# One recurrent branch on one core: unpadded products, a state in two buffers, and rows loaded ahead

## The chip, the core and the metric

The kernel is one program on one core of a Trainium2 chip. TensorE (PE in the profile) multiplies, VectorE (DVE), ScalarE (ACT) and GpSimd (POOL) do the rest, and SyncE (SP) issues most DMA transfers. The metric is the device time of one execution in microseconds (us); lower is better. The kernel before takes 3548.88 us, the median of 3 runs (3548.25 to 3555.68).

## The reference, cut to what matters

Two transformer-like blocks run one after the other. The change touches one branch of the first block, a recurrence over 1024 tokens with 8 heads of 64 columns. Each head keeps a 64x64 state:

```
def step(state, inp):                     # wkv7_scan, for each token
    r_t, w_t, k_t, kk_t, a_t, v_t = inp
    sa = einsum('bhvk,bhk->bhv', state, -kk_t)
    state = (state * w_t[:, :, None, :]
             + sa[..., None] * (kk_t * a_t)[:, :, None, :]
             + v_t[..., None] * k_t[:, :, None, :])
    return state, einsum('bhvk,bhk->bhv', state, r_t)
# around it: token shift, decay = exp(-exp(w_log)), a and g from small low-rank products,
# kk = normalised k*k_k, and behind it a group norm per head, a bonus term and the gate g
```

## The kernel before, in words

The program runs its phases one after the other, with a barrier between them: input projection, `rwkv` (this branch), attention, mixing, experts, and the second block. Only `rwkv` is changed, lines 1384 to 2017.

`rwkv` takes the 1024 tokens in 8 tiles of 128, and each tile as two chunks of 64. In a chunk the recurrence is solved in closed form: scores between the scaled rows of the chunk (`score`, L1897), then the inverse of a triangular 64x64 matrix for each head and chunk by squarings and blocks (`prod`, L1905: the names M, N, X, Z, XT, IN), then four steps with the state that must be done chunk after chunk: `state_rows` (L1858, L1859), `state_solve` (L1867), `state_step` (L1879, L1880) and `state_out` (L1887 to L1889). Behind them stand the group norm and the output on DVE (`centred`, `variance`, `output`).

The order is written out by hand for each engine. `body(t)` computes the scores and the inverse of tile t, and lays between them the state steps of tile t-1 (each of them for chunk 0 and for chunk 1) and the front work of tile t+1 (`lora_turn`, `lora_w`, `lora_a`, `lora_gate`, `sums`, `ends` on PE, with `decays` and `scale` on DVE and `exps` on ACT). Each engine runs its list in order and waits on step counters. `each_tile` makes body 0, then a hardware loop of 3 turns with two bodies each (tiles 1 to 6), then body 7; behind that the four state steps of tile 7 stand alone.

Four things matter for the change. The matmuls of `state_rows` and `state_out` contract over all 128 partitions: the state lies block-diagonally in `Sbd` with zeros between two heads, and the masked scores `Km`, `QB` and `QK` are 128 wide with zeros in the other chunk's half. DVE makes those masked scores with two 64-partition instructions each (L1730). SP loads the rows of tile t+2 behind the store of tile t-1's output, which waits for the end of that tile's norm (L1454 to L1466), and ACT reads the rows with `lora_in` (L1491) near the head of the next body. And ACT reloads its function table where two functions do not share one (ACT_TABLE_LOAD, 1.28 us each).

Of the kernel before, what the change touches and what calls it, by code (L numbers as in the profile page):

```python
# [15 lines left out]
P = 128  # L16
# [1344 lines left out]
CH = 64  # L1361
# [26 lines left out]
def rwkv(nc, xs_d, out, masks_d, g):  # L1388

    at, flat = rwkv_masks()  # L1390
    with Phase(nc, "rwkv") as ph:
# [13 lines left out]
        be, ka, vv, gg, lg, bg = (two(n, [P, RW]) for n in "be ka vv gg lg bg".split())  # L1405
# [3 lines left out]
        arT = two("arT", [P, 2, 4, P])  # L1409
        bkT = ph.sb("bkT", [P, 2, 4, P])  # L1410
# [15 lines left out]
        const_in, flat_in, x_in, o_st = (ph.sem(n) for n in ("const_in", "flat_in", "x_in", "o_st"))  # L1426
        passed = ph.sem("passed")
# [18 lines left out]
        FRONT, MIXED, STEP, OUT = 4, 5, 6, 7  # L1446

        @blk.sync
        def _(sp):
            def load(t, b):  # L1450
                sp.dma_start(xs[b][:, :], xs_d[bass.ds(t * P, P), :]).then_inc(x_in, 16)
# [5 lines left out]
            sp.dma_start(masks[:, :], masks_d).then_inc(flat_in, 16)  # L1457
            load(0, 0)
            for dst, src in ((wa2[0:64, :], g["rwkv_w2"]), (wa2[64:128, :], g["rwkv_a2"]), (g2[:, :], g["rwkv_g2"]),
                             (ind[:, :], g["ind64"])):  # L1460
                sp.dma_start(dst, src).then_inc(flat_in, 16)
            sp.sem_inc(o_st, 16)

            def store(t):
                sp.wait_ge(nd.sem, nd.at("out", t))
                sp.dma_start(out[bass.ds(t * P, P), :], yo[:, :, :].rearrange("p h d -> p (h d)")).then_inc(o_st, 16)  # L1466

            sp.wait_ge(x_in, 16)
            load(1, 1)
            for b in range(2):  # L1470
                free(b)
                load(b + 2, b)
                store(b)
            with sp.Fori(0, NT // 2 - 2) as j:
                for b in range(2):
# [3 lines left out]
            store(NT - 2)  # L1479
            store(NT - 1)  # L1480
            sp.wait_ge(o_st, 16 * (NT + 1))

        @blk.scalar
        def _(s):
            for dst, src in ((w0, g["rwkv_w0"]), (a0, g["rwkv_a0"]), (k_k, g["rwkv_k_k"]), (k_a, g["rwkv_k_a"]),
                             (r_k, g["rwkv_r_k"].rearrange("h d -> (h d)")), (ln_w, g["rwkv_ln_w"]), (ln_b, g["rwkv_ln_b"])):
                s.dma_start(dst, src.partition_broadcast(P)).then_inc(const_in, 16)

            def lora_in(t, b):
                s.wait_ge(x_in, 16 * t + 16)  # L1490
                s.activation(xs[b][:, 1536:1600], xs[b][:, 1536:1600], ACT.Sigmoid, scale=2.0)  # L1491
                s.activation(xs[b][:, 1664:1792], xs[b][:, 1664:1792], ACT.Sigmoid).then_inc(fa.sem, fa.step("lora_in"))
# [18 lines left out]
            def exps(t, b):  # L1511
# [12 lines left out]
            pair = lambda n: banks(ps, n)  # L1524
            flat2 = lambda z: z[:, :, :, :].rearrange("p a h c -> p (a h c)")
            one = lambda z: z[:, :, :].rearrange("p h c -> p (h c)")

            def state_copy(t, c, name, dst):
                s.wait_ge(sp_.sem, sp_.at(f"{name}{c}", t))
                s.activation(one(dst)[half(c), :], ps[half(c), STEP, :], ACT.Copy).then_inc(sa.sem, sa.step(f"{name}{c}"))  # L1530
# [9 lines left out]
            def body(t, b, n):  # L1540
                s.wait_ge(pe.sem, pe.at("turned", t))
                s.activation(arT[b][:, :, :, :].rearrange("p a i c -> p (a i c)"), pair(0), ACT.Copy)
                s.activation(bkT[:, :, :, :].rearrange("p a i c -> p (a i c)"), pair(2), ACT.Copy)\
                    .then_inc(act.sem, act.step("arT"))
                if not first(t):
                    state_copy(t - 1, 0, "r", Rs)
                if not last(t):
                    lora_in(t + 1, 1 - b)
                if not first(t):
                    state_copy(t - 1, 0, "u", Us)  # L1550
                evict(t, "mn2", flat2(MN2), pair(2))
                if not last(t):
                    square(t + 1)
                evict(t, "mn4", flat2(MN4), pair(1))
                if not last(t):
                    decays(t + 1)
                    gate(t + 1, 1 - b)
                    norm(t + 1)
                if not first(t):
                    state_copy(t - 1, 1, "r", Rs)  # L1560
                evict(t, "xx8", flat2(XX8), pair(1))
                if not first(t):
                    state_copy(t - 1, 1, "u", Us)
                evict(t, "z32", one(Z32), ps[:, 3, :])
                if not last(t):
                    if not first(t):
                        s.wait_ge(sd.sem, sd.at("s1", t - 1))
                    exps(t + 1, 1 - b)
                evict(t, "z64", one(Z64), ps[:, 2, :])
                if not first(t):  # L1570
                    norm_square(t - 1)
                    root(t - 1)
# [3 lines left out]
            lora_in(0, 0)  # L1576
            square(0)
            decays(0)
            gate(0, 0)
            norm(0)  # L1580
            exps(0, 0)
            each_tile(s, body)
# [7 lines left out]
        def _(po):  # L1590
            tt = po.tensor_tensor
            def body(t, b, n):
                po.drain()
                po.wait_ge(fd.sem, fd.at("scaled", t))
                po.wait_ge(pe.sem, pe.at("turned", t))
                po.sem_inc(passed, 1)
# [4 lines left out]
                po.drain()  # L1601
                if not first(t):
                    po.wait_ge(nd.sem, nd.start(t - 1))
                po.sem_inc(passed, 1)
                tt(lg[b][:, :], ln_w, gg[b][:, :], ALU.mult)
                po.drain()
                po.wait_ge(dve.sem, dve.at("bsum", t))
                po.sem_inc(passed, 1)
# [2764 lines left out]
```

## Time and profile before

| | us |
|---|---|
| median of 3 runs | 3548.88 |
| span of the profiled execution, first to last instruction | 3540.3 |
| what lies around the span, against the median | 8.6 |
| `rwkv` in the span, from its first DMA issue to the next phase's (515.4 to 955.3) | 439.9 |
| its start, until body 0 (515.4 to 549.0) | 33.6 |
| body 0 (549.0 to 585.4) | 36.4 |
| body 1 (585.4 to 628.6) | 43.2 |
| bodies 2 to 6 (628.6 to 879.9), 50.3 each | 251.3 |
| body 7, the last state steps and the barrier (879.9 to 955.3) | 75.4 |

A body is counted from its first transposes on PE (L1916) to those of the next. The profile has a row for each group of instructions with its start or its busy time; "busy" of PE counts modelled ends. PEclk is the granted share of TensorE's full clock. Over the whole span PE is busy 85%, DVE 54%, ACT 35%, POOL 20%.

### The profile page before, as it was taken

To read this page: it belongs to the slowest core of one execution; us is meant where nothing else is said; L and a number is where in the kernel's file an instruction comes from. 1 tells how busy PE (TensorE), PEld (TensorE's weight loads), DVE (VectorE), ACT (ScalarE), POOL (GpSimd) and SP (SyncE) were. 2 spreads that over 40 slices of the span, in tenths; PEclk is the share of its full clock that TensorE was granted. 3 is DMA by queue.
4 is the path that set the end of the run, shared out by engine and by line. 5 is a ranking of instruction groups with operands and counts; after the bars stand their busy time and mean duration, and the time that the engine had idled before them with its cause. 6 is when DMAs were issued, how large, how long until landed. Compare 5 with 4: busy or idle time off the path is not lost. (4 is left out here: it accounts for less than half of the span.)

```text
span 3540.3 us, 53898 instructions
## 1 busy us (share of the span) xinstructions
PE 3002.8 (85%) x21254; PEld 2570.1 (73%) x21254; DVE 1924.6 (54%) x2422; ACT 1255.0 (35%) x1768; POOL 696.0 (20%) x445
## 2 busy tenths in 40 slices
PE   7999977888668499389999987799999896868699
PEld 6999966777545388268887865699999874745487
DVE  3355735666357433468888865320067766665421
ACT  2000004344155322167777754221111155532311
POOL 3223301111055000212222201032223141220000
PEclk9999988888769699689999998899999998887899
DMA  4465330000121542489999965333466634031421
GB/s 163 145 215 200 114 123 13 29 30 16 70 24 60 210 165 90 155 299 399 399 399 398 399 249 199 129 129 103 153 198 219 207 120 151 4 137 38 173 95 47
DMA packets 258334, 572.38 MB, mean 162 GB/s; under 512 B 27920, under 2 KB 101632, under 8 KB 256560
## 3 DMA queue, kind: packets, MB, share of 16 engines
q1 hardware_dynamic: 208208, 450.29, 35.6%
q10 hardware_dynamic: 39344, 80.55, 6.1%
q0 software_dynamic: 10608, 39.13, 3.4%
q8 instruction: 120, 1.97, 0.2%
q14 instruction: 54, 0.44, 0.0%
HBM read 442.28 MB, written 126.45 MB: 161 GB/s over the span
## 5 line engine op out<-in xcount | busy, mean ns | idle before, releaser
L360 PE MATMUL pin_psum<-pin_sb_w,pin_sb_hT 128*128 128x354 f32 (+1 forms) x5376 | 978.5, 344 | 24.6 <-DVE pin_sb_w L322 20.0
L360 PEld LDWEIGHTS pin_psum<-pin_sb_w,pin_sb_hT 128*128 128x128 f32 x5376 | 934.8, 189 | 65.4 <-DVE pin_sb_w L322 20.8
L4170 DVE TENSOR_TENSOR moe_sb_wlo<-moe_sb_raw,moe_sb_whi 128x2048 fp32r<-128x2048 f32 x192 | 438.1, 2288 | 92.8 <-ACT moe_sb_whi L3995 92.6
L3995 ACT ACTIVATE moe_sb_whi<-moe_sb_raw 128x2048 fp32r<-128x2048 f32 x192 | 367.3, 1916 | 134.6 <-DMA moe_sb_raw<-in_w_gate 50.9
L294 ACT ACTIVATE pin_sb_xt<-pin_psum,pin_sb_ss 128x353 f32<-128x353 f32 (+1 forms) x112 | 63.5, 589 | 571.4 <-PE pin_psum L360 490.9
L339 DVE TENSOR_SCALAR pin_sb_xt<-pin_psum,pin_sb_ss 128x353 f32<-128x353 f32 (+1 forms) x112 | 69.0, 625 | 331.1 <-PE pin_psum L360 331.0
L4238 PE MATMUL moe_psum<-moe_sb_whi,moe_sb_xhi 128*128 128x512 f32 x512 | 204.3, 399 | 16.3 <-DVE moe_sb_xlo L4174 16.3
L251 POOL CAST pin_sb_w<-pin_sb_raw 128x2832 fp32r<-128x2832 f32 (+1 forms) x26 | 75.8, 2914 | 643.7 <-PE pin_psum L360 597.5
L4238 PE MATMUL moe_psum<-moe_sb_wlo,moe_sb_xhi 128*128 128x512 f32 x512 | 200.9, 392 | 0.0
L4238 PE MATMUL moe_psum<-moe_sb_whi,moe_sb_xlo 128*128 128x512 f32 x512 | 200.8, 392 | 0.0
L253 POOL TENSOR_TENSOR pin_sb_w<-pin_sb_raw,pin_sb_w 128x2832 fp32r<-128x2832 f32 (+1 forms) x26 | 186.1, 7157 | 3.9 <-issue 0.6
L4238 PEld LDWEIGHTS moe_psum<-moe_sb_whi,moe_sb_xhi 128*128 128x128 f32 x512 | 97.0, 189 | 41.9 <-issue 19.7
L3969 POOL COPY moe_sb_idx<-moe_sb_idx_all 128x1 int32 (+1 forms) x32 | 52.0, 1625 | 379.6 <-PE moe_psum L4227 377.4
L4238 PEld LDWEIGHTS moe_psum<-moe_sb_whi,moe_sb_xlo 128*128 128x128 f32 x512 | 97.0, 189 | 20.6
L4238 PEld LDWEIGHTS moe_psum<-moe_sb_wlo,moe_sb_xhi 128*128 128x128 f32 x512 | 97.2, 190 | 19.4
L4238 PE MATMUL moe_psum<-moe_sb_whi,moe_sb_ahi 128*128 128x512 f32 x256 | 103.3, 404 | 6.4 <-DVE moe_sb_alo L4178 6.4
L1327 PE MATMUL fin_psum<-fin_sb_whi,fin_sb_mhi 128*128 128x512 f32 x256 | 101.4, 396 | 5.9 <-DVE fin_sb_mlo L1285 5.9
L4238 PE MATMUL moe_psum<-moe_sb_whi,moe_sb_alo 128*128 128x512 f32 x256 | 101.0, 395 | 0.0
L4238 PE MATMUL moe_psum<-moe_sb_wlo,moe_sb_ahi 128*128 128x512 f32 x256 | 100.8, 394 | 0.0
L1327 PE MATMUL fin_psum<-fin_sb_whi,fin_sb_mlo 128*128 128x512 f32 x256 | 100.4, 392 | 0.0
L1327 PE MATMUL fin_psum<-fin_sb_wlo,fin_sb_mhi 128*128 128x512 f32 x256 | 100.3, 392 | 0.0
L3971 POOL DMA_INDIRECT moe_sb_xb<-scratch_hbuf,moe_sb_idx x32 | 81.3, 2541 | 33.7 <-issue 33.7
(701 smaller groups left out, 5890.9 us busy)
## 6 DMA issues: line engine op xcount, KB each, us to landing
moe_sb_raw<-in_w_gate SPq DMA_DIRECT2D x64, 1024.0 KB
moe_sb_raw<-in_w_up SPq DMA_DIRECT2D x64, 1024.0 KB, 14.0
moe_sb_raw<-in_w_down SPq DMA_DIRECT2D x64, 1024.0 KB, 13.0
pin_sb_raw<-in_w_in SPq DMA_DIRECT2D x16, 1412.0 KB, 8.1
scratch_proj<-pin_sb_xt ACTq DMA_DIRECT2D x16, 1412.0 KB, 7.4
pin_sb_raw<-in_w_in SPq DMA_DIRECT2D x12, 1792.0 KB, 8.9
scratch_proj<-pin_sb_xt ACTq DMA_DIRECT2D x12, 1792.0 KB, 6.5
scratch_ybuf<-moe_sb_yb ACTq DMA_DIRECT2D x32, 512.0 KB, 6.7
```

The costliest lines, as they stand in the source:

```text
L251: pool.tensor_copy(wt[b][0][:, :, :], raw[b][:, :, :])
L253: pool.tensor_tensor(wt[b][1][:, :, :], raw[b][:, :, :], wt[b][0][:, :, :].bitcast(F32), ALU.subtract)\
L294: a.activation(og[b][:, t, :], ps[:, t, 0:width], ACT.Copy, scale=ss[:, 3, t:t + 1]).then_inc(act_free, 1)
L339: v.tensor_scalar(og[b][:, t, :], ps[:, t, 0:width], ss[:, 3, t:t + 1], None, ALU.mult).then_inc(dve_free, 1)
L360: mm = te.matmul(ps[:, t, 0:cols], hT[a_part][:, k, t * P:(t + 1) * P], wt[b][w_part][:, k, :], start=(k == 0 and n == 0), stop=(k == KD - ...
L1327: mm = te.matmul(ps[:, 4 + 2 * b + h, :], m[:, k, :], w[:, k, h * 512:(h + 1) * 512], start=(k == 0 and i == 0), stop=(k == KM - 1 and i = ...
L3969: pool.tensor_copy(idx[b][:, :], idx_all[:, bass.ds(n, 1)] if not isinstance(n, int) else idx_all[:, n:n + 1])
L3971: pool.indirect_dma_start(out=xb[b][:, :], out_offset=None, in_=hbuf, in_offset=bass.IndirectOffsetOnAxis(ap=idx[b][:, :].bitcast(U32), ax ...
L3995: s.activation(whi[q][:, :, :], raw[q][:, :, :], ACT.Copy).then_inc(hi, 1)
L4170: tt(wlo[q][:, :, :], raw[q][:, :, :], whi[q][:, :, :].bitcast(F32), ALU.subtract).then_inc(lo, 1)
L4238: mm = te.matmul(out, xp[:, k, :], wp[q][:, w_at, :], start=(first and i == 0), stop=(last and i == 2))
```

## The change

Parts of it, each with its place:

- `state_rows` and `state_out` are split. `values_in` and `values_out` multiply the masked scores by the values; `state_rows`, `state_out` and `solved_out` take the rest. All are 64x64x64 matmuls, one for each head and chunk, and they add up in two PSUM banks that are sorted by the parity of the head (`zone`). `values_in(t-1)` stands near the head of body t, ahead of the state chain. The output of both chunks is made in one go.
- The state is held in `Sst[0]` and `Sst[1]`, for the two chunks; `Sbd` and its two 64-partition writes for each chunk are gone, and so is the last tile's second `state_step` and `carried`.
- `Km`, `QB` (together `KQ`) and `QK` are 64 wide. ACT copies them out of PSUM, and POOL multiplies them by the masks in place (three instructions of 128x512). DVE's L1730 is gone, and so are eight memsets.
- Pairs of products are evicted one at a time (`n2`, `m2`, `n4`, `m4`, `x8`, `xt8`: 128x512 where `mn2`, `mn4`, `xx8` were 128x1024), `ab` and `rk` likewise have a counter each, and n2 and n4 come first.
- SP loads tile t+2 before it waits for the store of t-1, and ACT's `lora_in(t+2)` stands at the end of body t. On PE `lora_turn(t+1)` stands near the head of body t, `ends(t+1)` at its end.
- At the start the rows come in two pieces, and each engine waits for what it reads, not for all constants.
- The loops are written out: no hardware loop in `rwkv`.

The core of the diff:

```
-            def free(t):
-                sp.wait_ge(x_in, 16 * t + 32)
-                sp.wait_ge(pool.sem, pool.at("rk", t))
 ...
-            with sp.Fori(0, NT // 2 - 2) as j:
-                for b in range(2):
-                    free(2 * j + 2 + b)
-                    load(2 * j + 4 + b, b)
-                    store(2 * j + 2 + b)
+            for t in range(NT):
+                if t + 2 < NT:
+                    sp.wait_ge(x_in, 16 * t + 32)
+                    sp.wait_ge(pool.sem, pool.at("rk", t))
+                    load(t + 2)
+                if t:
+                    store(t - 1)
 ...
+                po.wait_ge(act.sem, act.at("kq", t))
+                tt(Km[b], Km[b], over(M["strict"], RH), ALU.mult)
+                tt(QB[b], QB[b], over(M["incl"], RH), ALU.mult)
+                po.wait_ge(act.sem, act.at("qk", t))
+                tt(QK[b][:, :, :], QK[b][:, :, :], over(M["incl"], RH), ALU.mult).then_inc(pool.sem, pool.step("masked"))
 ...
-            def blocked(t, stage, src, outs, step):
-                ve.wait_ge(pe.sem, pe.at(stage, t))
-                for dst, slot, m in outs:
-                    for c in range(2):
-                        o = half(c)
-                        ins = tt(dst[o, :, o].rearrange("p (q i) c -> p q i c", q=2), split(src, slot)[o], m24(m)[o], ALU.mult)
 ...
-                for h in range(RH):
-                    d = slice(h * CH, (h + 1) * CH)
-                    te.matmul(ps[o, OUT, d], arT[b][:, 1, h // 2, o], Sbd[c][:, h // 2, half(h % 2)], start=True, stop=False)
-                    te.matmul(ps[o, OUT, d], QB[b][:, hp(h), o], Us[:, h, :], start=False, stop=False)
-                    mm = te.matmul(ps[o, OUT, d], QK[b][:, hp(h), o], vv[b][:, d], start=False, stop=True)
+            def value_products(t, kind, lhs):
+                b = t % 2
+                for j in range(RH):
+                    h = 2 * (j % 4) + j // 4
+                    for c in range(2):
+                        o = half(c)
+                        mm = te.matmul(zone(c, kind, j), lhs[o, j, :], vv[b][o, h * CH:(h + 1) * CH],
+                                       start=(j % 4 == 0), stop=False)
 ...
+                for i in range(4):          # state_rows(t, c); state_out has both c inside
+                    for q in range(2):
+                        mm = te.matmul(zone(c, STEP, 4 * q + i), abT[b][half(q), 0, i, o], Sst[c][half(q), i, :], start=False,
+                                       stop=(i == 3))
 ...
             def body(t):                    # PE, second half
                 prod(3, N32, X8).then_inc(pe.sem, pe.step("z32"))
                 if more:
                     sums(t + 1)
                 if t:
                     state_solve(p, 1)
                 te.wait_ge(act.sem, act.at("z32", t))
                 prod(0, XT8, Z32).then_inc(pe.sem, pe.step("x32"))
                 if t:
                     values_out(p)
                 prod(1, Z32, XT8).then_inc(pe.sem, pe.step("xt32"))
                 if t:
                     state_out(p)
                 te.wait_ge(dve.sem, dve.at("x32", t))
                 prod(2, N64, X32).then_inc(pe.sem, pe.step("z64"))
                 if t:
                     solved_out(p)
                     state_step(p, 1)
```

The end of a body on PE before, from the last products of Z to the first head of `state_out`:

```order
L1905 MATMUL rwkv_psum<-rwkv_sb_XX,rwkv_sb_Z 64x64 x16
L1845 ISA
L1848 MATMUL rwkv_psum<-rwkv_sb_ind,rwkv_sb_wide 128x2 x4
L1987 REGISTER_ALU
L1905 MATMUL rwkv_psum<-rwkv_sb_X,rwkv_sb_N 64x64 x16
L1887 MATMUL rwkv_psum<-rwkv_sb_Sbd,rwkv_sb_arT 64x64
L1888 MATMUL rwkv_psum<-rwkv_sb_Us,rwkv_sb_QB 64x64
L1889 MATMUL rwkv_psum<-rwkv_sb_vv,rwkv_sb_QK 64x64
```

The last three rows stand 8 times there, once for each head, and again in the middle of the body for the other chunk. The same place on PE now:

```order
L1949 MATMUL rwkv_psum<-rwkv_sb_Z,rwkv_sb_XT 64x64 x16
L1870 MATMUL rwkv_psum<-rwkv_sb_vv,rwkv_sb_QK 64x64 x16
L1949 MATMUL rwkv_psum<-rwkv_sb_XT,rwkv_sb_Z 64x64 x16
L1923 MATMUL rwkv_psum<-rwkv_sb_Sst,rwkv_sb_rkT 64x64 x16
L1949 MATMUL rwkv_psum<-rwkv_sb_X,rwkv_sb_N 64x64 x16
L1933 MATMUL rwkv_psum<-rwkv_sb_Us,rwkv_sb_KQ 64x64 x16
L1912 MATMUL rwkv_psum<-rwkv_sb_Us,rwkv_sb_be 64x64 x2
L1914 MATMUL rwkv_psum<-rwkv_sb_vv,rwkv_sb_ka 64x64 x2
```

The 24 matmuls for each of two chunks have become three groups of 16 for both, and each group lies between products of the inverse. ACT before, from the last eviction of a body to the second state copy of the next:

```order
L1522 ACTIVATE rwkv_sb_Z<-rwkv_psum 128x512
L1533 ISA
L1534 ACTIVATE rwkv_sb_sqy<-rwkv_sb_yc 128x512
L1537 REGISTER_ALU
L1538 ACT_TABLE_LOAD
L1538 ACTIVATE rwkv_sb_gn<-rwkv_sb_gn 128x8
L1541 ISA
L1542 ACTIVATE rwkv_sb_arT<-rwkv_psum 128x1024
L1543 ACTIVATE rwkv_sb_bkT<-rwkv_psum 128x1024
L1529 ISA
L1530 ACTIVATE rwkv_sb_Rs<-rwkv_psum 64x512
L1490 ISA
```

The row behind the last of these is the table load of `lora_in` (L1491). ACT now, at the same place (`sqy` and `gn` are the norm of the tile before, `xs` is `lora_in`):

```order
L1541 ACTIVATE rwkv_sb_Z<-rwkv_psum 128x512
L1536 ACTIVATE rwkv_sb_pend<-rwkv_psum 128x8
L1504 ACT_TABLE_LOAD
L1504 ACTIVATE rwkv_sb_xs<-rwkv_sb_xs 128x64
L1505 ACTIVATE rwkv_sb_xs<-rwkv_sb_xs 128x128
L1550 ACTIVATE rwkv_sb_sqy<-rwkv_sb_yc 128x512
L1554 ACT_TABLE_LOAD
L1554 ACTIVATE rwkv_sb_gn<-rwkv_sb_gn 128x8
L1541 ACTIVATE rwkv_sb_abT<-rwkv_psum 128x1024
L1541 ACTIVATE rwkv_sb_rkT<-rwkv_psum 128x1024
L1545 ACTIVATE rwkv_sb_Rs<-rwkv_psum 64x512
L1541 ACTIVATE rwkv_sb_KQ<-rwkv_psum 128x1024
```

`lora_in` has moved from between the two state copies to ahead of the norm and of the first eviction, and ACT has one table load more in a body (for `decays`, further down).

## Rows read from the trace of the kernel before

**Rows 1.** Busy time by stretch; columns: stretch, length, then as the heading says.

```profile
core 0: us, PE busy (x) PEld busy (x) DVE busy (x) ACT busy (x) POOL busy (x), PEclk, DMA share, GB/s
515.40:549.00 33.60, 10.39 (x18) 4.25 (x18) 17.07 (x27) 8.56 (x14) 0.00 (x0) 0.50 0.41 136
549.00:585.40 36.40, 29.54 (x643) 24.90 (x643) 21.45 (x35) 15.99 (x22) 7.96 (x7) 0.82 0.08 28
585.40:628.60 43.20, 39.87 (x902) 35.20 (x899) 26.37 (x45) 17.10 (x26) 7.98 (x7) 0.96 0.01 3
628.60:879.90 251.30, 213.43 (x4492) 189.20 (x4490) 155.52 (x260) 97.60 (x142) 41.98 (x35) 0.88 0.08 26
879.90:955.30 75.40, 54.51 (x1140) 51.76 (x1136) 34.41 (x60) 14.51 (x22) 8.68 (x7) 0.84 0.04 12
```

**Rows 2.** PE's waits in bodies 2 to 6: us in total, times, longest.

```profile
PE rwkv_psum L1879 <- ACT rwkv_sb_Us L1530: 18.0, 5, 6.0
PE rwkv_psum L1905 <- DVE rwkv_sb_QK L1730: 7.3, 5, 1.9
PE rwkv_psum L1916 <- issue: 5.9, 2, 3.0
```

**Rows 3.** Timeline, head of body 4: start, us, engine, instruction, idle before it.

```profile
736.44 0.37 SPq L1466 DMA_DIRECT2D scratch_o_rwkv<-rwkv_sb_yo  x1
737.20 0.35 SPq L1451 DMA_DIRECT2D rwkv_sb_xs<-scratch_xs  x1
742.00 0.26 ACT L1491 ACTIVATE rwkv_sb_xs<-rwkv_sb_xs 128x64 f32<-128x64 f32 x1 [6.27 <-DMA rwkv_sb_xs<-scratch_xs]
745.62 1.97 PE L1905 MATMUL rwkv_psum<-rwkv_sb_M,rwkv_sb_N 64*64 64x64 f32 x32
747.28 1.72 PEld L1905 LDWEIGHTS rwkv_psum<-rwkv_sb_N,rwkv_sb_M 64*64 64x64 f32 x30
```

**Rows 4.** PE in body 1, state rows, products and solve, at full clock.

```profile
612.10 0.33 PE L1858 MATMUL rwkv_psum<-rwkv_sb_Sbd,rwkv_sb_arT 128*64 128x64 f32 x2
614.11 1.15 PE L1905 MATMUL rwkv_psum<-rwkv_sb_X,rwkv_sb_IN 64*64 64x64 f32 x32
615.09 1.10 PE L1905 MATMUL rwkv_psum<-rwkv_sb_IN,rwkv_sb_X 64*64 64x64 f32 x32
616.03 1.09 PE L1867 MATMUL rwkv_psum<-rwkv_sb_Rs,rwkv_sb_XF 64*64 64x64 f32 x16
```

**Rows 5.** PE, `state_out` of one chunk, first row of it and first behind it.

```profile
774.71 0.33 PE L1887 MATMUL rwkv_psum<-rwkv_sb_Sbd,rwkv_sb_arT 128*64 128x64 f32 x2
777.65 1.15 PE L1905 MATMUL rwkv_psum<-rwkv_sb_Z,rwkv_sb_XT 64*64 64x64 f32 x32
```

**Rows 6.** PE, the scores of M and N, two groups of 16.

```profile
833.96 0.69 PE L1897 MATMUL rwkv_psum<-rwkv_sb_arT,rwkv_sb_bkT 64*64 64x64 f32 x32 [0.54 <-ACT rwkv_sb_bkT L1543]
834.45 0.68 PE L1897 MATMUL rwkv_psum<-rwkv_sb_bkT,rwkv_sb_arT 64*64 64x64 f32 x32
```

**Rows 7.** POOL, DVE, ACT groups in the branch: busy us, mean ns, idle before.

```profile
L1605 POOL TENSOR_TENSOR rwkv_sb_lg<-rwkv_sb_rows,rwkv_sb_gg 128x512 f32<-128x512 f32 x8 | 10.2, 1277 | 4.0 <-DVE rwkv_sb_yo L1714 2.9 <-issue 1.1
L1730 DVE TENSOR_TENSOR rwkv_sb_Km<-rwkv_psum,rwkv_sb_masks 64x512 f32<-64x512 f32 x16 | 11.0, 689 | 2.8 <-PE rwkv_psum L1897 2.1
L1491 ACT ACT_TABLE_LOAD x7 | 9.0, 1283 | 0.1
L1542 ACT ACTIVATE rwkv_sb_arT<-rwkv_psum 128x1024 f32<-128x1024 f32 x8 | 8.1, 1015 | 12.0 <-PE rwkv_psum L1916 12.0
```

**Rows 8.** Timeline, end of the start: what PE and DVE waited for.

```profile
528.40 0.45 PE L1822 MATMUL rwkv_psum<-rwkv_sb_masks,rwkv_sb_xs 128*128 128x128 f32 x1 [21.20 <-DMA rwkv_sb_ind<-in_ind]
532.02 0.41 DVE L1634 TENSOR_SCALAR rwkv_sb_loT<-rwkv_psum,rwkv_sb_masks 128x128 f32<-128x128 f32 x1 [8.10 <-DMA rwkv_sb_rows<-in_rwkv_ln_b]
```

**Rows 9.** Timeline, body 7, which stands outside the loop.

```profile
895.25 0.34 PE L1897 MATMUL rwkv_psum<-rwkv_sb_arT,rwkv_sb_bkT 64*64 64x64 f32 x5 [1.00 <-issue]
897.12 1.97 PE L1905 MATMUL rwkv_psum<-rwkv_sb_X,rwkv_sb_MN 64*64 64x64 f32 x32 [1.54 <-issue]
```

More of the change, by code:

```diff
@@ L1538, in root, with body @@
                 s.activation(gn[:, 3, :], gn[:, 2, :], ACT.Sqrt).then_inc(na.sem, na.step("root"))
[L1540 to L1552, printed above, removed]
+            def body(t):
+                b, p = t % 2, t - 1
+                more = t + 1 < NT
+                evict(t, "ab", turned(abT[b]), banks(ps, 0))
+                evict(t, "rk", turned(rkT[b]), banks(ps, 2))
+                if t:
+                    state_copy(p, 0, "r", Rs)
+                evict(t, "kq", KQ[b][:, :, :, :].rearrange("p s (q i) c -> p s q (i c)", q=2),
+                      ps[:, 2:4, :].rearrange("p q (s c) -> p s q c", s=2))
+                if t:
+                    state_copy(p, 0, "u", Us)
+                evict(t, "qk", QK[b][:, :, :].rearrange("p (q i) c -> p q (i c)", q=2), ps[:, 0:2, 0:256])
+                evict(t, "n2", one(N2), ps[:, 3, :])
+                evict(t, "m2", one(M2), ps[:, 2, :])
+                if more:
@@ L1569, in body @@
+                if more:
+                    exps(t + 1)
                 evict(t, "z64", one(Z64), ps[:, 2, :])
-                if not first(t):
-                    norm_square(t - 1)
-                    root(t - 1)
+                if more:
+                    ends(t + 1)
+                if t + 2 < NT:
+                    lora_in(t + 2)
+                if t:
+                    norm_square(p)
+                    root(p)
             for c in (fa, act, sa, na):
                 c.begin(s)
-            lora_in(0, 0)
+            lora_in(0)
@@ L1577, in _ @@
             square(0)
             decays(0)
-            gate(0, 0)
+            gate(0)
             norm(0)
-            exps(0, 0)
-            each_tile(s, body)
+            exps(0)
+            ends(0)
+            lora_in(1)
+            for t in range(NT):
+                body(t)
             for c in range(2):
@@ L1983, in body @@
                 prod(0, XT8, Z32).then_inc(pe.sem, pe.step("x32"))
+                if t:
+                    values_out(p)
                 prod(1, Z32, XT8).then_inc(pe.sem, pe.step("xt32"))
+                if t:
+                    state_out(p)
+                te.wait_ge(dve.sem, dve.at("x32", t))
+                prod(2, N64, X32).then_inc(pe.sem, pe.step("z64"))
+                if t:
+                    solved_out(p)
+                    state_step(p, 1)
+                te.wait_ge(act.sem, act.at("z64", t))
@@ L2005, in _ @@
             ends(0)
-            each_tile(te, body)
-            t, b = NT - 1, 1
-            te.wait_ge(dve.sem, dve.at("xf", t))
-            te.sem_inc(passed, 1)
-            for c in range(2):
-                state_rows(t, b, c)
-                state_solve(t, b, c)
-                state_step(t, b, c)
-                if not c:
-                    te.wait_ge(nd.sem, nd.start(t))
-                    te.sem_inc(passed, 1)
-                state_out(t, b, c)
+            for t in range(NT):
+                body(t)
+            p = NT - 1
+            te.wait_ge(dve.sem, dve.at("xf", p))
+            values_in(p)
+            state_rows(p, 0)
+            state_solve(p, 0)
+            state_step(p, 0)
+            state_rows(p, 1)
+            state_solve(p, 1)
+            values_out(p)
+            state_out(p)
+            solved_out(p)
 AH = 4
```

517 lines of the change are left out of this document (262 added, 255 removed).

## The prediction

> **What bounds it now.** I read first where the busy time lies by stretch [rows 1], then PE's waits [rows 2], then the timeline around the longest of them [rows 3]. In bodies 2 to 6 PE is busy 213.4 of 251.3 us, DVE 155.5, ACT 97.6, POOL 42.0: PE sets the pace, and what counts is PE's work and PE's waits. The waits are 251.3 − 213.4 = 37.9 us. The view of waits gives 18.0 to `state_step` waiting for ACT's copy of the solved rows, in five waits of up to 6.0; 7.3 to the masked scores of DVE; 5.9 to two restarts of the hardware loop. That leaves 6.7, or 1.3 a body.
>
> The first is not ACT's slowness. The timeline shows the chain: SP issues the store of the last tile's output at 736.44, only then the load of the next rows at 737.20, and ACT stands idle 6.27 us in `lora_in` until 742.00 [rows 3]. The copy that PE wants is queued behind `lora_in`. The long form comes in every second body.
>
> The clock is the third thing. PEclk is 0.96 in body 1, which hardly waits, and 0.88 in bodies 2 to 6 [rows 1]. Full-clock work is 213.4 × 0.88 / 5 = 37.6 us a body; at 0.96 the five bodies would be busy 195.8 instead of 213.4. So the stalls cost 17.6 us more by the clock that follows them. Behind the long stall 32 passes of products take 747.28 − 745.62 = 1.66 us [rows 3], against 615.09 − 614.11 = 0.98 in body 1 [rows 4]: the lower of the two levels, 1.2 GHz, against 2.4.
>
> **PE's work.** Removed in a body, at full clock: `state_rows` twice, 614.11 − 612.10 = 2.01 each [rows 4], and `state_out` twice, 777.65 − 774.71 = 2.94 each [rows 5]: 9.9 us. Added: `values_in`, `values_out` and `solved_out`, 16 matmuls each whose operands stand in both halves of the rows like those of `prod`, 0.98 each [rows 4]; `state_out`, 16 matmuls, and `state_rows`, 8 for each of two chunks. A group of 16 that spreads over four quarters takes 834.45 − 833.96 = 0.49 [rows 6], and one that does not spread so takes at most the price of `prod`, 0.98. So `state_out` costs 0.5 to 1.0 and each `state_rows` as much; together the added work is 4.4 to 5.9, and I take 5.0, since the quarter form is written for `state_rows` (q alternates). PE: −4.9 a body, 37.6 to 32.7.
>
> The Trainium skill, *TensorEngine Tiling (Array Packing)*, section "Gotcha 1: PSUM Pressure", says that different row tiles cannot use the same PSUM bank at a time. The new groups write both row halves of a bank. The products of [rows 4] do it too and show no turn-taking. By the row the sum is as above; by the rule the three groups would take twice as long, which is a rival below.
>
> **PE's waits.** The load is now issued ahead of the store, a whole body before `lora_in`, which itself stands at the end of a body: the 18.0 go, and no wait takes their place there, since the copy of the solved rows has only ready work ahead of it. The 7.3 go with `KQ` and `QK`: they are used a body later, so POOL's masks are never awaited. The loop's 5.9 go with the loop. What is late next is the first eviction of a body (`abT`). ACT has ahead of it, once the last product is out, two table loads of 1.28 and then `abT` of 1.02 [rows 7], with six small functions between them (0.26 for one of `lora_in` [rows 3]), some 5.0 us in all; PE has the transposes, `lora_turn` and `values_in`, about three groups of 1.0 [rows 4]: it waits 1.9. With the 1.3 of today's small waits and 1.4 for evictions that are now taken singly, 4.6 a body (bounds: 2.5, where ACT is ahead; 7, where `Rs` is late as well).
>
> The clock without long stalls: body 1 has it, 0.96. So a body is 32.7 / 0.96 + 4.6 = 38.7 us, and bodies 2 to 6 take 193.3 instead of 251.3: **−58.0**.
>
> **The other engines.** POOL gains three masks of 128x512 a body, at 1.28 by the nearest row [rows 7]: 42.0 / 5 = 8.4 goes to 12.2 of 38.7 us, covered by a body's distance to the reader. If POOL were late by a whole body PE would wait for it like for ACT; it is idle two thirds of the time. While POOL works, DVE's instructions with two operands in SBUF may stretch: between 0 and 0.8 a body, off PE's path. DVE loses six instructions of 0.69 [rows 7], 4.1 us. ACT gains a table load of 1.28 and evictions of 1.02 and 0.6: 19.5 a body goes to about 24, beside PE; its one price is the wait above. SP issues the same transfers in another order.
>
> **Around it.** Body 1 falls from 43.2 to 38.7: −4.5. Body 0 (36.4) has no state work; DVE's 4.1 us and the waits for the masks stand on its path, since PE is busy 29.5 there [rows 1]: 2 to 7, I take −5. The start: PE stands until 528.40 for `ind`, DVE until 532.02 for the last of seven broadcast rows [rows 8]; now four rows come first, at about 526.5 if the seven land evenly: −5.5 (2 to 8). Body 7 and the tail, 75.4 at 0.84 [rows 1]: 4.9 / 0.84 = 5.8 of PE work, 2 of waits, and behind the body two `state_out` of 2.94 / 0.84 = 7.0 together become 2.9 for both chunks, with one `state_step` of about 1 less: −13 (8 to 16).
>
> Sum: 58.0 + 4.5 + 5.0 + 5.5 + 13.0 = 86.0. The profiled span is 3540.3, and 3540.3 − 86.0 = 3454.3; with the 8.6 around it, which is the distance to the median of the runs shown, 3462.9. Forecast **3463**.
>
> **Rivals.**
> - *The clock stays at 0.88.* The waits of 4.6 are spread, but the gate may not forgive them; for it speaks body 7's 0.84, against it body 1. 32.7 / 0.88 = 37.2 instead of 34.1, +15.5, and some 5 in the other bodies: 3483.
> - *Straight code stalls in fetching.* Body 7, outside the loop, has idle times of 1.00 and 1.54 that only `issue` ends [rows 9]. At 2.5 for each of 8 bodies: +20, 3483. The Trainium skill, *Runtime: NRT & Kernel Launch*, section "Instruction fetch mechanics", holds that sequential prefetch hides the fetch and a taken branch breaks it: the restarts of up to 3.0 [rows 2] agree, body 7 does not. By it this term would be nothing, as in the forecast.
> - *Groups in one bank take turns.* The three new groups 1.9 instead of 0.98 each: 2.8 / 0.96 × 8 = +23, 3486. Against it: the products [rows 4]. The skill's rule above stands for it.
> - *The load doesn't come early.* It still waits for POOL's `rk` of tile t; if that is as late as the norm, 18 stays and half of the clock's 17: 3490.
> - *More.* Clock 1.0 (34.1 to 32.7 a body, −11 in 8) and ACT ahead of PE (2.9 instead of 4.6, −14): 3438.
> - *Slower.* All of PE's work in the branch is now in 64x64 quarters with short gaps; should the clock stay on its lower level, work stretches by 1.66 / 0.98 = 1.7: 32.7 × 1.7 + 4.6 = 60.2 against 50.3, +50 in five bodies and +25 in the rest: 3624. It decides below a mean clock of 0.72 (32.7 / 0.72 + 4.6 = 50.0). For it: the stretch behind the stall; against it: body 1.
>
> **How the numbers follow.** Forecast 58%; clock 14%; fetching 7%; turns 4%; load 3%; more 11%; slower 3%. The range takes in all but the last and the outer ends: start and tail can be 9 less, `state_rows` 0.9 a body more, waits 2.4 a body more, not all together: 3434 to 3500. A measurement tells about 0.2%, 7 us, from no change. Faster 0.96, same 0.01, slower 0.03.
>
> **What the profile after would show.** Bodies of 38 to 39 us; PEclk at 0.95 or more in bodies 2 to 6; PE busy 34 a body; no wait of `state_step` for `Us` above 1 us, no idle time of ACT ahead of `lora_in`; a wait of PE for `abT` of 2 us at each head; three PE groups of 1.0 us where six and a half stood; POOL near 12 us a body and never a releaser of PE; DVE's first work before 528. I am wrong if bodies are over 42 us, if ACT's evictions release PE for over 6 us a body, or if PEclk stays below 0.9.

## The result, and the profile after

The changed kernel takes 3451.07 us (median of 4 runs, 3447.60 to 3460.30) against 3548.57 for the kernel before run beside it: ratio 0.9736, interval 0.9714 to 0.9757, that is 86 to 101 us less. The forecast was 3463 with 3434 to 3500 around it.

| | before | after |
|---|---|---|
| span of the profiled execution | 3540.3 | 3446.8 |
| ahead of the branch | 515.4 | 511.2 |
| **the branch** | **439.9** | **342.8** |
| its start | 33.6 | 27.3 |
| body 0 | 36.4 | 32.6 |
| body 1 | 43.2 | 34.3 |
| bodies 2 to 6 | 251.3 (50.3 each) | 187.2 (37.4 each) |
| body 7 and the tail | 75.4 | 61.5 |
| behind the branch | 2585.0 | 2592.7 |

All of the gain lies in the branch: 97.1 us. The parts before and behind it, whose code is the same, differ by 4 and 8 us; behind the branch, the profiles of this case lie between 2585 and 2599 us. So small effects are read below from the length of the branch, from the first transfer of its rows to the first of attention's. The same kernel profiled twice gave 342.8 and 342.7 there; every other kernel below has one profile.

The first view is the busy time by stretch of the changed kernel, with the columns of [rows 1]; the stretches are the start, body 0, body 1, bodies 2 to 6, and the rest:

```profile
511.20:538.48 27.28, 10.45 (x18) 4.25 (x19) 9.98 (x18) 10.04 (x17) 0.00 (x0) 0.50 0.53 168
538.48:571.12 32.64, 28.15 (x642) 23.92 (x643) 20.95 (x29) 15.13 (x24) 13.09 (x10) 0.87 0.10 31
571.12:605.40 34.28, 33.40 (x899) 29.52 (x900) 23.41 (x34) 19.08 (x30) 13.09 (x10) 0.95 0.09 31
605.40:792.57 187.17, 168.25 (x4493) 146.02 (x4492) 138.37 (x211) 111.70 (x170) 61.42 (x50) 0.96 0.09 30
792.57:854.06 61.49, 41.85 (x1106) 39.53 (x1105) 26.54 (x45) 16.82 (x28) 11.77 (x10) 0.78 0.04 15
```

Against [rows 1], bodies 2 to 6 have 168.25 us of PE work instead of 213.43, idle time of 18.9 instead of 37.9, and a clock of 0.96 instead of 0.88. POOL has 61.4 where it had 42.0.

PE's waits in bodies 2 to 6, in answer to [rows 2]: total, times, longest.

```profile
PE rwkv_psum L1941 <- ACT rwkv_sb_abT L1541: 6.7, 5, 1.5
PE rwkv_psum L1941 <- DVE rwkv_sb_N L1742: 4.9, 5, 1.0
PE rwkv_psum L1859 <- DVE rwkv_sb_Sst L1755: 2.9, 5, 0.9
PE rwkv_psum L1949 <- DVE rwkv_sb_IN L1747: 1.6, 5, 0.3
```

The waits for `Us` and for the masked scores and the loop restarts are gone. The two that lead now both stand at the head of a body: for the eviction `abT` of ACT and for the masks of N of DVE.

PE's timeline in body 4 shows the prices; each duration is read from a row's start to the next group's, as in [rows 4 to 6]:

```profile
685.33 0.57 PE L1894 MATMUL rwkv_psum<-rwkv_sb_Sst,rwkv_sb_abT 64*64 64x64 f32 x13
685.79 0.58 PE L1941 MATMUL rwkv_psum<-rwkv_sb_abT,rwkv_sb_rkT 64*64 64x64 f32 x28
...
709.16 1.09 PE L1870 MATMUL rwkv_psum<-rwkv_sb_vv,rwkv_sb_QK 64*64 64x64 f32 x31
710.05 1.03 PE L1949 MATMUL rwkv_psum<-rwkv_sb_XT,rwkv_sb_Z 64*64 64x64 f32 x29
710.98 0.67 PE L1923 MATMUL rwkv_psum<-rwkv_sb_Sst,rwkv_sb_rkT 64*64 64x64 f32 x30
711.70 1.15 PE L1949 MATMUL rwkv_psum<-rwkv_sb_X,rwkv_sb_N 64*64 64x64 f32 x32
712.68 0.93 PE L1933 MATMUL rwkv_psum<-rwkv_sb_Us,rwkv_sb_KQ 64*64 64x64 f32 x26
```

`state_rows` takes 685.79 − 685.33 = 0.46, `values_out` 0.9, `state_out` 0.7 with a short wait for DVE behind it, a product group 0.98.

The head of body 5 (from 717.07) on ACT and DVE, with the two waits of PE:

```profile
717.44 1.28 ACT L1504 ACT_TABLE_LOAD   x1
717.99 0.69 DVE L1715 TENSOR_TENSOR rwkv_sb_yc<-rwkv_psum,rwkv_sb_gn 128x512 f32<-128x512 f32 x1
719.10 0.61 ACT L1550 ACTIVATE rwkv_sb_sqy<-rwkv_sb_yc 128x512 f32<-128x512 f32 x1
719.75 0.69 DVE L1721 TENSOR_REDUCE rwkv_sb_gn<-rwkv_sb_sqy 128x8 f32<-128x512 f32 x1 [1.06 <-ACT rwkv_sb_sqy L1550]
721.05 0.21 ACT L1554 ACTIVATE rwkv_sb_gn<-rwkv_sb_gn 128x8 f32<-128x8 f32 x1
721.17 1.01 ACT L1541 ACTIVATE rwkv_sb_abT<-rwkv_psum 128x1024 f32<-128x1024 f32 x1
722.23 1.16 PE L1941 MATMUL rwkv_psum<-rwkv_sb_abT 64*64 64x64 f32 x64 [1.47 <-ACT rwkv_sb_abT L1541]
723.80 0.69 DVE L1738 TENSOR_TENSOR rwkv_sb_yo<-rwkv_sb_yc,rwkv_sb_bg 128x512 f32<-128x512 f32 x1
725.71 0.68 DVE L1742 TENSOR_TENSOR rwkv_sb_M<-rwkv_psum,rwkv_sb_masks 128x512 f32<-128x512 f32 x1
726.31 1.88 DVE L1742 TENSOR_TENSOR rwkv_sb_N<-rwkv_psum,rwkv_sb_masks 128x512 f32<-128x512 f32 x3
728.24 1.03 PE L1941 MATMUL rwkv_psum<-rwkv_sb_rkT 64*64 64x64 f32 x28 [0.98 <-DVE rwkv_sb_N L1742]
```

The norm of the tile before goes to and fro between DVE and ACT, and both `abT` and the masks of M and N are queued behind it. ACT has no idle time here from 717.25 until `abT` is done; a second table load, for the norm's root, ends at 721.01, when DVE's part of the norm is also just done.

At the start, in answer to [rows 8], DVE's `loT` (first row) no longer waits for any of the constants' rows, and DVE's next long wait is for the large part of `xs`, which `direction` reads (second row). The branch begins at 511.2 here, so these are 7.4 and 12.6 us behind its beginning; in [rows 8] `loT` stood 16.6 behind it.

```profile
518.61 0.41 DVE L1657 TENSOR_SCALAR rwkv_sb_loT<-rwkv_psum,rwkv_sb_masks 128x128 f32<-128x128 f32 x1 [6.97 <-PE rwkv_psum L1831]
523.80 0.69 DVE L1662 TENSOR_TENSOR rwkv_sb_wide<-rwkv_sb_xs,rwkv_sb_rows 128x512 f32<-128x512 f32 x1 [4.59 <-DMA rwkv_sb_xs<-scratch_xs]
```

### The profile page after: what moved, and what is told of

Same layout as the page of the kernel before. It is cut to its first block and busy times, and to the rows that moved or that the text cites. A ratio compares the mean times of both kernels' runs of the same rounds, so it can differ in the third digit from the quotient of the medians.

```text
span 3446.8 us, 53114 instructions
## 1 busy us (share of the span) xinstructions
PE 2940.3 (85%) x21222; PEld 2515.3 (73%) x21222; DVE 1892.7 (55%) x2331; ACT 1274.5 (37%) x1810; POOL 727.1 (21%) x469
## 6 DMA issues: line engine op xcount, KB each, us to landing
moe_sb_raw<-in_w_gate SPq DMA_DIRECT2D x64, 1024.0 KB, 12.3
```

## The experiments

Six of the eleven runs ask where the 97 us come from, two whether POOL and the place of `values_in` matter, two try the waits at the head, one repeats the changed kernel. "Branch" is its length in the profile. Each ratio is to the kernel before as it ran beside that kernel.

| kernel | time, us | ratio to before, interval | branch | bodies 2 to 6: length, PE busy, clock |
|---|---|---|---|---|
| before | | | 439.9 | 251.3, 213.4, 0.88 |
| after | 3451.07 | 0.9736, 0.9714 to 0.9757 | 342.8 | 187.2, 168.3, 0.96 |
| before, load ahead | 3529.76 | 0.9948, 0.9931 to 0.9964 | 427.4 | 238.3, 209.1, 0.91 |
| the same, loops written out | 3525.46 | 0.9944, 0.9927 to 0.9960 | 418.1 | 231.3, 208.5, 0.92 |
| after, masks on DVE in six pieces | 3472.35 | 0.9805, 0.9777 to 0.9833 | 368.7 | 204.6, 173.9, 0.92 |
| after, masks on DVE in three | 3455.60 | 0.9743, 0.9727 to 0.9760 | 349.9 | 190.6, 170.9, 0.96 |
| after, with stalls | 3460.11 | 0.9763, 0.9747 to 0.9780 | 358.6 | 203.8, 175.0, 0.92 |
| after, more PE work | 3483.29 | 0.9833, 0.9800 to 0.9866 | 373.3 | 204.9, 186.9, 0.96 |
| after, POOL's masks twice | 3453.00 | 0.9739, 0.9714 to 0.9764 | 341.8 | 186.6, 169.3, 0.95 |
| after, values late | 3447.33 | 0.9730, 0.9706 to 0.9754 | 341.9 | 187.5, 168.6, 0.95 |
| after, lora later | 3448.30 | 0.9729, 0.9706 to 0.9751 | 340.7 | 187.0, 165.5, 0.98 |
| after, again | 3454.45 | 0.9746, 0.9730 to 0.9761 | 342.7 | 187.0, 168.0, 0.96 |
| after, norm split | 3428.32 | 0.9677, 0.9660 to 0.9694 | 321.4 | 169.1, 162.1, 1.00 |

**The load ahead, in the kernel before.**

```
                 for b in range(2):
                     free(2 * j + 2 + b)
                     load(2 * j + 4 + b, b)
-                    store(2 * j + 2 + b)
+                    store(2 * j + 1 + b)
```

> The kernel before with one thing changed: SP issues the load of tile t+2 ahead of the store of tile t-1 (lora_in stays near the head of the body, the hardware loop and all work of PE stay). Theory, load and clock: ACT's idle time ahead of lora_in goes, with it PE's 18.0 us of state_step waiting for Us, and the granted clock of bodies 2 to 6 rises from 0.88 to 0.94 or more, which is worth another 10 to 17 us: 28 to 35 us in all, 3514 to 3521. Rival one, no clock: the waits go and the clock stays at 0.88: 16 to 19 us, about 3531. Rival two, the next wait is right behind: under 8 us.

PE's waits in bodies 2 to 6:

```profile
PE rwkv_psum L1907 <- DVE rwkv_sb_QB L1732: 9.6, 5, 2.3
PE rwkv_psum L1907 <- DVE rwkv_sb_QK L1732: 7.0, 5, 1.9
PE rwkv_psum L1918 <- issue: 6.5, 2, 3.2
PE rwkv_psum L1899 <- DVE rwkv_sb_N L1722: 2.2, 3, 0.9
```

The wait for `Us`, 18.0 in [rows 2], is gone altogether, as every theory had it. But the one for QB has grown from 2.2 to 9.6 and that for N from 0.8 to 2.2: half of the stall came back as a wait for DVE's masks, which the stall had hidden. The clock rose to 0.91, not to 0.94. The branch is 12.4 us shorter: bodies 2 to 6 gave 13.0 and the tail 3.4, but bodies 0 and 1 took 2.6 and 1.5 more. In body 0 the granted clock was 0.72 instead of 0.82, though PE's work there is the same; no run explains it. None of the three is right as written: the time (13 to 24 us less) takes in that of rival one, but the way is a part of the theory and a part of rival two.

**The loops written out on top of it.** The edit replaces `each_tile` and POOL's loop by `for t in range(NT)`, and SP's loop by a plain `for` over the same steps, so that all bodies stand one behind the other in the program.

> As the last, and the loops of all engines in this branch written out. Theory: the restarts of 5.9 us go, 5 to 8 us below the last kernel (with the clock a little more). Rival, fetching: straight code stalls as in body 7 of the kernel before, with idle times of 1.0 to 1.5 us that end by issue in each body: 5 us or more above the last kernel.

The branch is 9.3 us shorter than that of the last kernel; the ratio alone couldn't have shown it. Of this 7.0 lie in bodies 2 to 6, where the two restarts had taken 6.5. Another 2.1 lie in body 0, which never was in the loop: its clock is back at 0.82. So the loops themselves are worth about 7, as the theory had it. The rival looks half right in the waits of this kernel, where PE's idle time is ended by `issue` in straight code:

```profile
PE rwkv_psum L1905 <- DVE rwkv_sb_QB L1729: 8.4, 5, 2.1
PE rwkv_psum L1905 <- issue: 3.4, 3, 1.6
...
PE rwkv_psum L1905 <- DVE rwkv_sb_QK L1729: 2.8, 2, 1.4
```

One more of the same kind stands in body 1, and its timeline shows what it is:

```profile
598.02 1.39 DVE L1729 TENSOR_TENSOR rwkv_sb_QK<-rwkv_psum,rwkv_sb_masks 64x512 f32<-64x512 f32 x2
599.50 0.69 DVE L1638 TENSOR_TENSOR rwkv_sb_wide<-rwkv_sb_xs,rwkv_sb_rows 128x512 f32<-128x512 f32 x1
599.51 1.15 PE L1905 MATMUL rwkv_psum<-rwkv_sb_X,rwkv_sb_MN 64*64 64x64 f32 x32 [1.65 <-issue]
```

The masks of QK end at 598.02 + 1.39 = 599.41 and PE starts 0.1 later: a wait for DVE, which the view has put down to `issue`. The three in bodies 2 to 6 (0.3, 1.6 and 1.5 us) also end 0.1 us behind DVE's second piece of QK. The long one of [rows 9] is of the same kind. In the kernel before, DVE's two pieces of QK stand at

```profile
895.63 1.39 DVE L1730 TENSOR_TENSOR rwkv_sb_QK<-rwkv_psum,rwkv_sb_masks 64x512 f32<-64x512 f32 x2 [0.21 <-PE rwkv_psum L1897]
```

and end at 897.02, with PE starting at 897.12 [rows 9]. The other row of [rows 9], 1.00 us in the middle of a group, has no such partner. There is one of 1.1 us in this kernel's five bodies and none in the changed kernel's. What it is stays open.

**The masks back on DVE.** Both kernels are the changed one without ACT's two copies and POOL's three products.

```
+                ve.wait_ge(pe.sem, pe.at("kq", t))
+                masked(Km[t % 2], 2, 0, "strict")          # or both halves apart
+                masked(QB[t % 2], 2, 1, "incl").then_inc(dve.sem, dve.step("kq"))
                 ve.drain()
                 tt(X1[:, :, :], M1[:, :, :], m8("eye"), ALU.add).then_inc(dve.sem, dve.step("x1"))
+                ve.wait_ge(pe.sem, pe.at("qk", t))
+                masked(QK[t % 2], 0, 0, "incl").then_inc(dve.sem, dve.step("qk"))
```

> The changed kernel, with the masks of KQ and QK done by DVE straight out of PSUM (three instructions of 128x512 in a body, 0.69 us each) and neither ACT's two copies nor POOL's three products. Theory, masks belong off DVE: PE waits at the first squaring for the two instructions on KQ and again at x2 for QK, some 1.5 to 2.5 us a body: 10 to 20 us slower than the changed kernel, 3461 to 3471. Rival: DVE and PE have room, and ACT's 1.6 us fewer in a body cover it: within 5 us of the changed kernel, 3446 to 3456.

> As the kernel with the masks on DVE, but each of the three done as the kernel before does it, in two instructions of 64 partitions (six of 0.69 us in a body instead of three). Theory, what the change gained by the masks is DVE's instruction count: 2.1 us more of DVE in each body ahead of X1 and X2, and PE waits for most of it: branch 350 to 360 to 366, that is 10 to 16 us over the three-instruction form. Rival: DVE still has room, since it is busy 29 of 37 us and what is late is the norm: within 4 us of 350.

In three pieces the branch grows by 7.1 us, between the theory and the rival. This rests on the branch in one profile: the interval of the ratio overlaps that of the changed kernel. In six, the form of the kernel before, it grows by another 18.8, over the theory's 10 to 16, and body 0 takes 36.4, as long as in the kernel before. The waits of the latter in bodies 2 to 6:

```profile
PE rwkv_psum L1952 <- DVE rwkv_sb_KQ L1739: 7.9, 5, 1.6
PE rwkv_psum L1944 <- DVE rwkv_sb_N L1734: 7.8, 5, 1.6
PE rwkv_psum L1944 <- ACT rwkv_sb_abT L1541: 7.3, 5, 1.5
```

So of the 26 us that the masks are worth, 19 come from writing them in one instruction instead of two halves (which needs the unpadded form) and 7 from the other engine. DVE was busy 160.6 of 204.6 us there: an engine with a fifth of its time free was still what PE waited for.

**Stalls put back.** The copies are placed where PE's only way on is behind them.

```
+                if t in (2, 4, 6):
+                    for _ in range(10):
+                        s.activation(junk[:, :], w0, ACT.Copy)
+                        s.drain()
                 evict(t, "kq", ...
```

> The changed kernel, with ten copies of 128x512 (some 6.3 us) that nobody reads on ACT ahead of the eviction of KQ in bodies 2, 4 and 6. Theory, the clock follows the stalls: PE stands some 5 us in each of the three, and the clock behind them falls, so that the branch grows by the waits of about 15 us and by 5 to 12 us more of PE busy time; granted clock of bodies 2 to 6 from 0.96 to 0.92 or less. Rival: only the waits, 13 to 17 us, and the clock stays at 0.95.

```profile
605.77:809.52 203.75, 174.97 (x4492) 152.32 (x4492) 137.76 (x211) 129.52 (x200) 61.91 (x50) 0.92 0.08 27
...
PE rwkv_psum L1954 <- ACT rwkv_sb_KQ L1542: 11.3, 3, 4.6
```

Bodies 2 to 6 are 16.6 us longer: idle time grew by 9.9 (28.8 instead of 18.9) and PE's busy time by 6.7, with the same 4492 matmuls, at 0.92. The branch as a whole grew by 15.8, which by its length alone would fit the rival; but the clock and the slower work are those of the theory, and what it had too large are the waits, 15 for 9.9. To 1 us of idle time came 0.7 of slower work. This is what the prediction took from two stretches of one profile (17.6 us for the clock), now with the work unchanged.

**More PE work.**

```
+                for _ in range(4):
+                    for j in range(RH):
+                        for c in range(2):
+                            te.matmul(zone(c, OUT, j), QK[t % 2][half(c), j, :], vv[t % 2][half(c), j * CH:(j + 1) * CH],
+                                      start=True, stop=True)
                 value_products(t, OUT, QK[t % 2]).then_inc(fresh, 1)
```

> The changed kernel with four more groups of 16 64x64 products in each state_out (they write the output zone and are overwritten): PE work of some 3.9 us at full clock, about what the change took out. Theory, PE sets the pace: each microsecond of PE counts, 3.9 / 0.96 = 4.1 us in each of 7 bodies and the tail, branch 343 to 372 to 378. Rival: the change's smaller PE work is worth less than itself, since waits for ACT and DVE shrink when PE is slower: under 20 us, branch below 363.

```profile
610.11:815.05 204.94, 186.90 (x5133) 165.27 (x5132) 137.62 (x211) 111.70 (x170) 60.96 (x50) 0.96 0.08 28
```

32 groups in all cost 30.5 us, 0.95 each; in bodies 2 to 6 PE's busy time grew by 18.7 and the length by 17.8. PE's work counts about one for one, and a group whose two row halves write one bank at a time, each its own half of the partitions, costs what [rows 4] says. This run's rival falls, and so does the prediction's of groups that take turns in a bank.

**POOL's masks twice, and the values late.**

```
+                po.drain()
+                tt(Km[b], Km[b], over(M["strict"], RH), ALU.mult)     # QB and QK likewise
```

> The changed kernel with POOL's three mask products done twice (a product with ones and zeros, so the values stay): POOL's work goes from 12.3 to 16 or 17 us a body. Theory, POOL is covered by the body between the masks and their reader: the branch stays within 2 us of 343, POOL releases PE nowhere; a few DVE instructions with two operands in SBUF get longer. Rival: rk and bonus of POOL are behind the masks, and DVE's bsum or output waits: 5 us or more.

The branch is 341.8: no price, though POOL was busy 82.5 us of 186.6 in bodies 2 to 6. The cover holds.

```
-                if t:
-                    values_in(p)
                 te.wait_ge(act.sem, act.at("ab", t))
                 score(0, 0, beT, alT)
                 score(0, 1, alT, beT).then_inc(pe.sem, pe.step("mn"))
                 if t:
+                    values_in(p)
                     state_rows(p, 0)
```

> The changed kernel with values_in behind the first scores instead of ahead of the wait for abT. Theory: values_in covers 1.0 us of the wait for abT, so PE waits 1.0 us longer at each head in bodies 1 to 7, and state_rows is as late: branch 5 to 8 us longer, 348 to 351. Rival: the later start is made good at the next wait (n64), under 2 us.

PE waits 12.7 us for `abT` in bodies 2 to 6 instead of 6.7, and there no longer for N: the work moved from one wait into the next. The branch is 341.9. The rival is right, and the place of the value products ahead of the state chain is worth nothing here.

**The head of a body, twice.** First the small front work is taken out of it. ACT's part is shown; `lora_turn` and `lora_w` on PE and `lora_turned` and `direction` on DVE move back likewise.

```
-                if t + 2 < NT:                 # ACT, end of the body
-                    lora_in(t + 2)
...
                 evict(t, "kq", ...
+                if more:
+                    lora_in(t + 1)
```

> The changed kernel with the small front work of the next tile taken out of the head of a body: ACT's lora_in(t+1) stands behind the eviction of KQ instead of ahead of abT, PE's lora_turn and lora_w stand between the first products, DVE's lora_turned and direction behind X1. Theory, the head is bound by what ACT and DVE have queued there: PE's 1.3 us a body for abT and 1.0 for the masks of N go, some 2 us a body: branch 343 to 329 to 335 us, time 3437 to 3444. Rival: the two chains are only moved, and the bias on DVE or the copy of Us now comes late: branch 340 us or more.

The branch is 2.1 us shorter, and the waits that were to go grew: `abT` to 8.7, N to 8.1. The head of its body 5 (from 715.97) shows why:

```profile
717.61 0.63 ACT L1550 ACTIVATE rwkv_sb_sqy<-rwkv_sb_yc 128x512 f32<-128x512 f32 x1 [1.29 <-DVE rwkv_sb_yc L1714]
718.27 0.69 DVE L1720 TENSOR_REDUCE rwkv_sb_gn<-rwkv_sb_sqy 128x8 f32<-128x512 f32 x1 [0.69 <-ACT rwkv_sb_sqy L1550]
719.55 0.21 ACT L1554 ACTIVATE rwkv_sb_gn<-rwkv_sb_gn 128x8 f32<-128x8 f32 x1
719.67 1.00 ACT L1541 ACTIVATE rwkv_sb_abT<-rwkv_psum 128x1024 f32<-128x1024 f32 x1
```

With `lora_in` gone ACT idles 1.29 us for the norm, whose own chain (DVE's centring, ACT's square, table load and root) still ends at 719.76. `abT` starts 3.70 us behind the start of the body instead of 4.10, and PE, which has less to do ahead of it, waits longer. Then the norm is taken apart:

```
-                    root(p)                                # ACT: from the end of the body ...
                 state_copy(p, 0, "r", Rs)
+                if t >= 2:
+                    root(t - 2)                            # ... to behind Rs of the next
-                    output(p)                              # DVE: from the end of the body ...
                 added(t, "x2", "x2", 0, X2, X1[:, :, :])
+                if t >= 2:
+                    output(t - 2)                          # ... to behind X2 of the next
```

> The changed kernel with the norm of the tile before taken apart: centring, square and variance stay at the end of the body, ACT's root stands behind the copy of Rs and DVE's output behind X2 of the next body. Theory, the head of a body is bound by the ping-pong of the norm between DVE and ACT, not by lora_in: the wait for abT (6.7 in bodies 2 to 6) goes under 1.5 and that for N (4.9) under 1.0, about 2 us a body in six or seven bodies, and with fewer waits the clock is 0.97 or more: branch 324 to 332, time 10 to 18 us below the changed kernel. Rival: the output on DVE (3 us) now holds X4 or the rows of the next tile, and the waits come back there: branch above 338.

Bodies 2 to 6, the largest waits that are left in them, and attention's first transfer, where the branch ends:

```profile
605.88:774.95 169.07, 162.05 (x4493) 140.18 (x4492) 140.19 (x211) 111.14 (x170) 63.57 (x50) 1.00 0.10 33
...
PE rwkv_psum L1863 <- DVE rwkv_sb_Sst L1757: 2.9, 5, 0.9
PE rwkv_psum L1953 <- DVE rwkv_sb_IN L1749: 1.6, 5, 0.3
...
833.67 0.33 SPq L2136 DMA_DIRECT2D att_sb_ident<-in_ident  x1
```

Both waits are gone and nothing took their place; the clock is full, PE is busy 96%. The branch is 833.67 − 512.27 = 321.4 us, 21.3 shorter than that of the control beside it and below the theory's 324 to 332, with these terms: 12.0 us of idle time and 5.9 of busy time less in bodies 2 to 6, 2.8 less in the last stretch, although two norms now stand at its end, and 0.6 ahead of body 2. It is the fastest kernel of the case: 3428.32, its ratio 0.9660 to 0.9694 below the control's 0.9730 to 0.9761. The medians differ by 26 us, of which the 5 beyond the branch are within what the unchanged code varies by. The edit does two things at once: each engine finds its input ready, and less stands ahead of what PE waits for (on ACT a table load of 1.28 and the root, on DVE the output). The run doesn't tell the two apart.

> The changed kernel once more, as it is, beside the last one. The branch should come out at 343 within 2 us, the time within 4 us of 3451; this tells how far the branch and the time of one profile can be trusted.

The control came out at 342.7 and 3454.45, both within what was expected.

## Why the prediction was right

The sum was 86.0 us, the branch gave 97.1, and the mechanism is the one forecast. Term by term:

- **PE's work, −4.9 a body: −5.3.** Full-clock work was 37.6 and is 168.25 × 0.96 / 5 = 32.3. Of the added 5.0, `state_rows` was taken near its lower bound and has it, 0.46; `state_out` was in effect taken at 1.0 and takes 0.7, and `values_out` 0.9 for 0.98, which is about the 0.4. About one for one on the path, by the kernel with more PE work.
- **The wait for `Us`, 18.0:** gone, as forecast. But "no wait takes their place there" holds only with the masks moved too: by itself the load was worth 12.4 us, half of its stall coming back as DVE's masks. The parts of this change are not independent, and the prediction didn't say so.
- **The clock at 0.96:** right (0.96), and shown by the stalls put back.
- **4.6 us of waits a body:** 3.8. The one for `abT` was to be 1.9 and is 1.3; the one for N, 1.0, was in no term of its own. Its cause was half read: the table loads and `lora_in` that were counted ahead of `abT` do fill ACT until then, but the norm's path through DVE is just as long, so that taking `lora_in` away moved `abT` by 0.4 us only. And DVE's stretch beside POOL was put off PE's path, while it stands ahead of the masks of N (last section).
- **Bodies 2 to 6, −58.0: −64.1**, from less work and fewer waits than forecast. **Body 1, −4.5: −8.9.** This term was mis-sized by a plain mistake: it was given the waits of the others, but no norm of an earlier tile stands at its head, and PE is idle only 34.28 − 33.40 = 0.9 us.
- **Start −5.5: −6.3. Body 0 −5: −3.8. Tail −13: −13.9.** The start's size is luck. It was worked out from four rows landing before seven, but `loT` needs no row at all now and starts 9.2 us earlier against the beginning of the branch; DVE's next long wait is for `xs`. Body 0 is the masks, as forecast: with them on DVE in six pieces it is as long as before.
- **POOL never on the path:** right; 12.3 us a body as forecast, and with a third more still no price.
- **Of the rivals** the clock at 0.88, the turns in one bank, the late load and the slower case are refuted by rows above. "Straight code stalls in fetching" rested on a name in the profile: the longer of its two rows was a wait for DVE's masks of QK. The changed kernel, all straight code, has no wait of PE by `issue` in bodies 2 to 6, so the Trainium skill's rule in *Runtime: NRT & Kernel Launch*, section "Instruction fetch mechanics", which the prediction saw contradicted by body 7, agrees with this case: the restarts of up to 3.2 us went with the loop. Two rows of 1.0 and 1.1 us in straight code stay open. "More" was half right: the time was 12 us below the forecast, by waits and work rather than by the clock.

How the parts add up: 6.3 for the start, 12.4 for the load, 9.3 for the loops, 25.9 for the masks (undone in the changed kernel), and 5.3 / 3.9 × 30.5 = 41.4 for PE's work, scaled from the kernel with more of it: 95.3 of 97.1. The last is an estimate, since the old form of the products was not put back alone; with the 18.7 × 0.96 / 5 = 3.6 that bodies 2 to 6 measured instead of 3.9 it is 44.9, and the sum 98.8. That the sum comes so near is in part luck, since the load and the loops were measured on the old kernel, the masks and PE's work on the new one, and the parts lean on each other. The evictions taken singly and the state in two buffers have no run of their own. The time as a whole came out 12 under the forecast by 11 us more in the branch; the differences of 4 and 8 us in the code around it, and 4.3 instead of 8.6 us around the span, nearly cancel.

## What to carry to other kernels

When the longest wait goes, look at once for what it had hidden: here taking away a stall of 18 us gave 12 alone, since half of it came back as waits for DVE's masks; with these shortened as well nothing took its place. Where two engines pass a small chain to and fro (here a norm), the chain as a whole delays everything queued behind it on both, and taking other work out of its way gave only 2 us; moving its steps apart, behind what the busy engine waits for, gave 21. And where a wait is put down to `issue`, look for an instruction on another engine that ends 0.1 us before.

## What the runs showed of the hardware

- The granted clock falls with short waits too, and comes back when they end: with 18.9 us idle in 187 it was 0.96, with 28.8 in 204 it was 0.92, with 7.0 in 169 it was 1.00. Ending 12 us of waits of 1.0 to 1.5 gave 6 us more by the clock. The sum of idle time alone doesn't set it: the kernel with lora later had 21.5 us idle in 187 (187.0 less 165.5) and 0.98, the old kernel with its loops written out 22.8 in 231 and 0.92. What makes the difference isn't known.
- An operation of DVE with both operands in SBUF took up to 1.76 us beside POOL's products, and 0.69 where POOL is idle. The same line in the changed kernel, in body 5 and body 7 beside one of POOL's products, and at the end, where POOL is idle:

```profile
721.14 1.27 POOL L1628 TENSOR_TENSOR rwkv_sb_bon<-rwkv_sb_bon,rwkv_sb_rows 128x512 f32<-128x512 f32 x1
721.57 1.38 DVE L1732 TENSOR_TENSOR rwkv_sb_yc<-rwkv_sb_yc,rwkv_sb_gn 128x512 f32<-128x512 f32 x1
...
796.68 1.76 DVE L1732 TENSOR_TENSOR rwkv_sb_yc<-rwkv_sb_yc,rwkv_sb_gn 128x512 f32<-128x512 f32 x1
...
848.85 0.69 DVE L1732 TENSOR_TENSOR rwkv_sb_yc<-rwkv_sb_yc,rwkv_sb_gn 128x512 f32<-128x512 f32 x1
```

It may well have had a price here. In body 5 DVE has no idle time from this row (721.57) to the end of the masks of N (728.19), and PE waits 0.98 us for these until 728.24. So up to 1.38 − 0.69 = 0.69 us of that wait is the stretch, by estimate; no run takes the stretch away alone.
